# Staged queries, whole values and an earlier place for the first keys in the second attention's loads

## The chip, the cores and the metric

The kernel runs on one core of one Trainium2 chip. The metric is the device time of one execution in microseconds. Three runs of the kernel before gave 2737.96, 2739.23 and 2741.26 us, so its median is 2739.23 us. Lower is better.

## The reference

The program is a network of two blocks over 1024 tokens of width 1024, all in fp32. The first block is a short-convolution layer and a stick-breaking attention layer. The second block, which the change concerns, is this (cut):

```
h = rmsnorm(x) * (1 + scale1) + shift1
qa, ka, va, qd, kd, vd, ga, gd = split(h @ w_in)     # 512,128,128,512,512,512,1024,1024 columns
# sliding window attention: 8 query heads, 2 key/value heads, head size 64, window 128
scores = qa . ka * 64**-0.5 - slope * distance;  softmax with a sink logit;  out_a = probs . va
# differential attention: 4 heads, two score maps each, value size 128
a = softmax(map 0) - lam * softmax(map 1);  out_d = rmsnorm(a . vd) * (1 - lam_init)
x = x + gate1 * ((sigmoid(ga) * (out_a @ w_branch_swa) + sigmoid(gd) * (out_d @ w_branch_diff)) @ w_out)
```

After it come a feed-forward part with a causal convolution, and a last rmsnorm.

## The kernel before, in words

Activations lie transposed, features on the partitions and tokens along the row. A product in fp32 is made of three passes of two rounded parts: each operand is split into a high and a low part, and high x high, low x high and high x low are added in PSUM. So most tensors exist twice, as part 0 (high) and part 1 (low).

**The projections of the second block (`U_IN2`).** The first four column blocks are ordinary products. The thirty others are made in 15 blocks i = 0 to 14 of two units (row 0 and row 1), each by seven products of half-size matrices, in TensorE's order P1, P2, P6, P5, P7, P4, P3. ScalarE takes copies of PSUM between them (`snap`, L2324): number 0 after P1, number 1 after P6, number 2 after P7. P6 waits for copy 0, P7 for copy 1, and P3 waits for a sum of VectorE (L3017) that reads copy 2. ScalarE's whole order is written out by hand in `in2_act`: it also makes the high parts of the weights (L2296) and of the results (`in2_use`, L2358), and it issues the stores of the results (`in2_store`, L2370 and after) on its own DMA queue. VectorE makes the low part of a result (`in2_low`, L3028) before its store.

The queries are units 0 to 7 in storing order. Units of the four ordinary products are stored first: in `in2_act` two calls of `in2_store(-2, row)` stand together ahead of `snap(0, 2)`, and two calls of `in2_store(-1, row)` together ahead of `snap(1, 0)`. The query units 4 to 7 are stored in blocks 1 and 2, row 0 ahead of `snap(i, 2)` and row 1 behind it. Each store writes one part of one unit, [128, 1024], into `q2_dram[part, 128 rows, :]`; a unit's 128 rows are two heads of 64. Before the stage of `in2_use` is written again it waits for the stores of the same row.

**The second attention.** TensorE, ScalarE, VectorE and GpSimd walk through 16 steps of sliding window attention (a head and a half of the tokens each: step x is head x // 2, half x % 2) and then 32 steps of differential attention. In step t, TensorE makes the scores of step t (L854), turns the probabilities of step t - 2 (L893) and multiplies those of step t - 3 with the values (L912). VectorE makes the minimum and the biased scores of step t (L1152) and after them the norm of step t - 1 (L1204). ScalarE makes the exponentials (L1029).

The queries of head pair c lie in `opA[:, e, c, :]`, e being the head of the pair. The upper 64 partitions hold the low part and the lower 64 the high part, and the keys (`keys[slot][part]`) hold the same 64 rows twice, so that one matmul over 128 partitions adds two of the three passes. The values of key/value head g are wanted in a form with 128 columns a block, one half of them zero: head n reads `vals[2 * g + n % 2]`, in which the values stand in half n % 2 and the other half is zero (written by GpSimd, L1669, in `second_pool`).

**The queue of loads.** All loads of this attention are issued by SyncE in the order of `second_loads`, on one queue. It waits for P1 of the last block, issues the first half of the tokens of pairs 0 to 3 (L684, 16 transfers of 64 partitions), waits for P7 of the last block and a low weight of VectorE, issues two pieces more, the first keys (`dup`, L638, four transfers of 64 partitions and 4 KB a row) and the values (L663, two transfers in pieces of 64 numbers), then waits for P4, and issues the other second halves. The keys and values of group 1, the queries of the differential heads and their keys follow. TensorE's step 0 waits for the first half of pair 0 and for the first keys, its step 1 for the second half of pair 0 (`q_half`, L843). Gates are stored by ScalarE (L2377) in the same stretch, on the other queue.

Of the kernel before, what the change touches and what calls it, by code (L numbers as in the profile page):

```python
# [10 lines left out]
F32 = mybir.dt.float32  # L11
# [5 lines left out]
P = 128  # L17
T = 1024
D = 1024
# [275 lines left out]
def program(nc, a, out, known):  # L295
# [3 lines left out]
    with ctx:  # L299
# [10 lines left out]
        def at(name, offset, shape, dt=F32):  # L310
            return nc.alloc_sbuf_tensor_at(name, [P] + shape, dt, offset=offset)
# [67 lines left out]
        def scratch(name, shape, dt=F32):  # L379
            return nc.dram_tensor(name, shape, dt).ap()  # L380
# [2 lines left out]
        k_dram = scratch("k_dram", [2, D, T])  # L383
        q_dram = scratch("q_dram", [2, D, T])
        v_dram = scratch("v_dram", [KC, P, T])
        q2_dram = scratch("q2_dram", [2, D, T])
        k2_dram = scratch("k2_dram", [2, D, T])
        va_dram = scratch("va_dram", [P, T])
        vd_dram = scratch("vd_dram", [DIFF_HEADS, P, T])
# [182 lines left out]
        def now(s):  # L572

            return total.get(id(s), 0)

        def step(s, *name, by=1):

            total[id(s)] = now(s) + by
            if name:
                names[name] = now(s)  # L580
# [52 lines left out]
        def second_loads(sp):  # L633
            def dup(slot, hf, rows, name, cols_of):

                for part in range(2):
                    for place in range(2):
                        sp.dma_start(keys[slot][part][place * DH:(place + 1) * DH, cols_of].bitcast(F32),  # L638
                                     k2_dram[part, rows, cols_of]).then_inc(k_in[slot][hf], 16)
                        step(k_in[slot][hf], *name, by=16)  # L640

            def diff_keys(q):
                j, m = diff_map(q)
                slot = key_slot(q)
                if q == 1:
                    sp.wait_ge(pe_done, at("seven", U_IN2, LAST_IN2, P3))
                elif q < 3:
                    sp.wait_ge(pe_done, at("sec_S", 4 * q + 7, 0))
                else:
                    former, fm = diff_map(q - 3)  # L650
                    sp.wait_ge(pe_done, at("sec_S", SWA_STEPS + NT * former + NT - 1, fm))
                rows = slice((1 + j) * P + m * DH, (1 + j) * P + m * DH + DH)
                for hf in range(2):
                    dup(slot, hf, rows, ("k_in", "diff", q, hf), slice(hf * HALF, (hf + 1) * HALF))

            def swa_keys_values(g):
                if g:
                    sp.wait_ge(pe_done, at("seven", U_IN2, LAST_IN2, P3))
                dup(g, 0, slice(g * DH, (g + 1) * DH), ("k_in", "swa", g), slice(0, T))
                for e in range(2):  # L660
                    dst = vals[2 * g + e][:].rearrange("p (b s d) -> p b s d", b=NT, s=2)[:, :, e, :]
                    src = va_dram.rearrange("p (b s d) -> p b s d", b=NT, s=2)[:, :, g, :]
                    sp.dma_start(dst, src).then_inc(v_in[g], 16)  # L663
                    step(v_in[g], "v_in", "swa", g, by=16)

            def diff_value(j):
                x = 8 * j + 7
                sp.wait_ge(pe_done, at("sec_pv", x, second_pieces(x) - 1))
                sp.dma_start(vals[2 * (j % 2)][:], vd_dram[j]).then_inc(v_in[j % 2], 16)
                step(v_in[j % 2], "v_in", "diff", j, by=16)  # L670

            def queries(c):

                for e in range(2):
                    for part in range(2):
                        sp.dma_start(opA[part * DH:(part + 1) * DH, e, c, :].bitcast(F32),
                                     q2_dram[part, c * P + e * DH:c * P + (e + 1) * DH, :]).then_inc(q_in[c], 16)
                        step(q_in[c], "q_in", c, by=16)

            def query_half(c, e, hf):  # L680

                t = slice(hf * HALF, (hf + 1) * HALF)
                for part in range(2):
                    sp.dma_start(opA[part * DH:(part + 1) * DH, e, c, t].bitcast(F32),  # L684
                                 q2_dram[part, c * P + e * DH:c * P + (e + 1) * DH, t]).then_inc(q_half[c][hf], 16)
                    step(q_half[c][hf], "q_half", c, hf, by=16)

            def branch_weights(n):

                u = U_BRANCH + n  # L690
                for w, col0, row0, chunks, k0 in source(u):
                    src = w[row0:row0 + chunks * P, col0:col0 + P].rearrange("(k p) n -> p k n", p=P)
                    sp.dma_start(branch_raw(n)[:, k0:k0 + chunks, :], src).then_inc(w_in[u % 2], 16)
                    step(w_in[u % 2], "w_in", u, by=16)


            sp.wait_ge(in2_stored[0], at("in2_stored", U_IN2 + 16))
            sp.wait_ge(in2_stored[1], at("in2_stored", U_IN2 + 17))
            sp.wait_ge(pe_done, at("seven", U_IN2, LAST_IN2, P1))
            for c in range(4):  # L700
                for e in range(2):
                    query_half(c, e, 0)
            sp.wait_ge(pe_done, at("seven", U_IN2, LAST_IN2, P7))
            sp.wait_ge(dve_done, at("seven_w", U_IN2, LAST_IN2, P3))
            query_half(0, 0, 1)
            swa_keys_values(0)
            sp.wait_ge(pe_done, at("seven", U_IN2, LAST_IN2, P4))
            query_half(0, 1, 1)
            for c in range(1, 4):
                for e in range(2):  # L710
                    query_half(c, e, 1)

            sp.wait_ge(pe_done, at("seven", U_IN2, LAST_IN2, P3))
            swa_keys_values(1)
            for j in range(DIFF_HEADS):
                queries(4 + j)
            diff_keys(1)
            diff_keys(0)
            diff_value(0)
            diff_keys(2)  # L720
            for row in range(2):
                sp.wait_ge(in2_stored[row], at("in2_stored", in2_unit(LAST_IN2, row)))
            for n in range(2):
                branch_weights(n)
            for n in EARLY_GATES:
                sp.dma_start(gates[:, n, :], gate_dram[n]).then_inc(gates_in, 16)
                step(gates_in, "gates_in", by=16)
            for j in range(1, DIFF_HEADS):
                diff_value(j)
                diff_keys(2 * j + 1)  # L730
                if j < DIFF_HEADS - 1:
                    diff_keys(2 * j + 2)
# [797 lines left out]
        def _(pool):  # L1530
# [106 lines left out]
            def second_pool():  # L1637
# [22 lines left out]
                for g in range(2):  # L1660
                    if g:
                        pool.wait_ge(pe_done, at("seven", U_IN2, LAST_IN2, P3))
                    else:
                        pool.wait_ge(pe_done, at("seven", U_IN2, LAST_IN2, P5))
                        pool.wait_ge(dve_done, at("seven_w", U_IN2, LAST_IN2, P3))
                    for e in range(2):
                        other = vals[2 * g + e][:].rearrange("p (b s d) -> p b s d", b=NT, s=2)[:, :, 1 - e, :]
                        pool.wait_ge(pool_done, now(pool_done))
                        pool.memset(other, 0.0).then_inc(pool_done, 1)  # L1669
                        step(pool_done, "val_zero", g)  # L1670

                row = bias[:, 0, :]
                pool.wait_ge(dve_done, at("sec_p", SWA_STEPS - 2, 0))
# [414 lines left out]
        def _(act):  # L2088
# [272 lines left out]
            def in2_store(i, row):  # L2361

                u = in2_unit(i, row)
                n = in2_place(u)
                act.wait_ge(act_done, at("in2_used", u))
                if in2_kind(u) == "parts":
                    act.wait_ge(dve_done, at("in2_lo", u))
                    dram, row0 = (q2_dram, n * P) if n < 8 else (k2_dram, (n - 8) * P)
                    for part in range(2):
                        act.dma_start(halves_of(dram[part, row0:row0 + P, :]), in2_stage(row, part).bitcast(F32)).then_inc(in2_stored[row], 16)  # L2370
                        step(in2_stored[row], "in2_stored", u, by=16)
                elif in2_kind(u) == "value":
                    dst = va_dram if n == 13 else vd_dram[n - 14]
                    act.dma_start(halves_of(dst), in2_plain(row)).then_inc(in2_stored[row], 16)
                    step(in2_stored[row], "in2_stored", u, by=16)
                else:
                    act.dma_start(halves_of(gate_dram[n - 18]), in2_plain(row)).then_inc(in2_stored[row], 16)  # L2377
                    step(in2_stored[row], "in2_stored", u, by=16)
# [891 lines left out]
```

## Time and profile before

| what | value |
|---|---|
| median of 3 runs | 2739.23 us (2737.96 to 2741.26) |
| profiled execution, its own time | 2738.89 us |
| its span | 2737.1 us |
| mean granted TensorE clock | 0.978 |
| PE (TensorE) busy | 2598.2 us, 95% of the span |
| DVE (VectorE) busy | 1531.7 us, 56% |
| ACT (ScalarE) busy | 1109.5 us, 41% |
| POOL (GpSimd) busy | 857.6 us, 31% |
| queue q1 (SyncE's) | 303.91 MB, 37.3% of 16 engines' span |
| queue q10 (ScalarE's) | 68.69 MB, 6.7% |

Busy time is an average over stages with different limits. Whether an edit counts is read from the place where it lies: which wait ends last there. "ACTq" and "SPq" in a row are the sequencers of ScalarE and SyncE issuing a DMA. While a sequencer issues, the instructions behind it on its engine stand. The number in square brackets is the time that the engine sat idle before the instruction, with the one that released it.

### The profile page before, as it was taken

How to read it: one execution, taken by the hardware profiler on the slowest of the kernel's cores; microseconds unless marked ns; L12 is line 12 of the kernel's file. 1: busy time of each engine (PE TensorE's matmuls, PEld its weight loads, DVE VectorE, ACT ScalarE, POOL GpSimd, SP SyncE). 2: the span in 40 equal slices, each digit the busy share in tenths (PEclk: the TensorE clock that was granted, in tenths of full speed). 3: DMA queues.
4: the chain of work that ended last, by engine and by line, in shares of the span. 5: the costliest groups of instructions: out<-in, count | busy, mean ns of one | idle time of the engine just before them, and what ended most of it. 6: DMA issues, size and time to landing. Idle time of an engine off the chain costs nothing.

```text
span 2737.1 us, 34710 instructions
## 1 busy us (share of the span) xinstructions
PE 2598.2 (95%) x12391; PEld 2161.8 (79%) x12391; DVE 1531.7 (56%) x2083; ACT 1109.5 (41%) x1865; POOL 857.6 (31%) x627
## 2 busy tenths in 40 slices
PE   6999999999899999999899988889997999999998
PEld 4888887788788899987688878668776888887887
DVE  5665665630424566657853438766578777771112
ACT  5200102511410688846544437661265555551000
POOL 2233331032232566620222220333101322325664
PEclk8999999999999999999999999999998999999999
DMA  6344444262455544434353346414242333338833
GB/s 242 100 142 136 143 134 123 77 222 86 146 197 168 126 111 109 112 119 154 103 176 115 109 149 169 152 32 169 85 131 93 102 115 108 108 106 306 288 94 122
DMA packets 377272, 374.81 MB, mean 137 GB/s; under 512 B 36323, under 2 KB 284556, under 8 KB 376972
## 3 DMA queue, kind: packets, MB, share of 16 engines
q1 hardware_dynamic: 346844, 303.91, 37.3%
q10 hardware_dynamic: 30256, 68.69, 6.7%
q8 instruction: 99, 1.62, 0.3%
q14 instruction: 73, 0.60, 0.1%
HBM read 286.55 MB, written 85.98 MB: 136 GB/s over the span
## 4 chain that ended last, share of the span: by engine, by line
PE 76%; DVE 12%; ACT 4%; DMA 3%; issue 1%; SPq 1%; POOL 1%; ACTq 0%; DVEq 0%; POOLq 0%
PE PS L1773 28%; PE PS L1861 20%; PE PS L1930 8%; PE PS L810 5%; PE PS L1820 3%; PE PS L788 2%; PE PS L2001 2%; DMA mod_raw<-in_w_ada 1%; PE PS L774 1%; PE PS L773 1%; DVE prob L1185 1%; PE PS L1843 1%; PE PS L1975 1%; DVE M L2659 1%; DVE Xr L2981 1%
## 5 line engine op out<-in xcount | busy, mean ns | idle before, releaser
L1773 PE MATMUL PS<-opA,w_hi 128*128 128x512 f32 x2176 | 680.2, 392 | 3.0 <-POOL w_lo L1579 3.0
L1773 PEld LDWEIGHTS PS<-opA,w_hi 128*128 128x128 f32 x2176 | 411.1, 189 | 89.3 <-POOL w_lo L1579 3.4
L1773 PE MATMUL PS<-opA,w_lo 128*128 128x512 f32 x1088 | 425.4, 391 | 0.0
L1574 POOL CAST w_hi<-w_raw 128x1024 fp32r<-128x1024 f32 (+1 forms) x117 | 123.4, 1055 | 793.2 <-PE PS L1773 448.2
L1861 PE MATMUL PS<-opB,Xr 128*128 128x512 f32 x1120 | 312.1, 396 | 17.4 <-ACT M L2324 17.4
L1579 POOL TENSOR_TENSOR w_lo<-w_raw,w_hi 128x1024 fp32r<-128x1024 f32 (+1 forms) x118 | 285.2, 2417 | 34.8 <-ACT w_hi L2203 25.4
L1861 PE MATMUL PS<-opA,Xr 128*128 128x512 f32 x980 | 277.2, 393 | 6.2 <-ACT M L2324 3.0
L1861 PEld LDWEIGHTS PS<-opB,Xr 128*128 128x128 f32 x1120 | 214.7, 192 | 64.2 <-ACT M L2324 18.6
L2659 DVE SCALAR_TENSOR_TENSOR M<-mod_raw,small,M 128x512 f32<-128x512 f32 x168 | 177.6, 1057 | 139.5 <-DMA mod_raw<-in_w_ada 80.4
L1773 PEld LDWEIGHTS PS<-opA,w_lo 128*128 128x128 f32 x1088 | 205.6, 189 | 42.4 <-issue 0.2
L1861 PEld LDWEIGHTS PS<-opA,Xr 128*128 128x128 f32 x980 | 183.0, 188 | 50.1 <-ACT M L2324 8.3
L2943 DVE SCALAR_TENSOR_TENSOR X<-PS,mod,X 128x512 f32<-128x512 f32 x64 | 48.0, 751 | 293.8 <-PE PS L1930 206.5
L1861 PE MATMUL PS<-opA,w_first 128*128 128x512 f32 x840 | 197.8, 391 | 5.6 <-ACT M L2334 5.6
L1861 PEld LDWEIGHTS PS<-opA,w_first 128*128 128x128 f32 x840 | 158.8, 189 | 39.1 <-ACT M L2334 6.0
L1747 POOL TENSOR_TENSOR X<-w_raw 128x512 f32<-128x512 f32 x36 | 48.4, 1344 | 380.0 <-DVE xn L2732 228.2
L1773 PE MATMUL PS<-opB,w_hi 128*128 128x512 f32 x512 | 161.4, 394 | 5.4 <-DVE opB L2931 3.0
L1129 DVE TENSOR_TENSOR_SCAN M<-PS,beta 128x896 f32<-128x896 f32 (+7 forms) x86 | 116.4, 1359 | 69.7 <-ACT PS L1005 55.8
L3017 DVE TENSOR_TENSOR M<-M,PS 128x512 f32<-128x512 f32 x140 | 96.3, 688 | 101.0 <-ACT M L2324 66.1
L2981 DVE TENSOR_TENSOR Xr<-X,Xr 128x512 fp32r<-128x512 f32 x140 | 116.9, 835 | 63.4 <-ACT Xr L2296 55.2
L1930 PE MATMUL PS<-opA,w_hi 128*128 128x512 f32 x480 | 149.3, 389 | 0.0
L2219 ACT ACTIVATE squares<-X 128x512 f32<-128x512 f32 x48 | 30.4, 633 | 236.8 <-DVE X L2943 233.6
L2324 ACT ACTIVATE M<-PS 128x512 f32<-128x512 f32 x105 | 62.8, 598 | 151.8 <-PE PS L1861 127.8
(266 smaller groups left out, 4777.5 us busy)
## 6 DMA issues: line engine op xcount, KB each, us to landing
mod_raw<-in_w_ada SPq DMA_DIRECT2D x96, 256.0 KB, 2.9
z_dram<-opB ACTq DMA_DIRECT2D x44, 512.0 KB, 3.9
w_raw<-in_a_w_in SPq DMA_DIRECT2D x32, 512.0 KB, 4.5
hin<-q_dram SPq DMA_DIRECT2D x64, 256.0 KB, 6.0
w_raw<-in_w_down SPq DMA_DIRECT2D x32, 512.0 KB, 3.9
opA<-z_dram SPq DMA_DIRECT2D x60, 256.0 KB, 5.3
mod_raw<-in_b_mod_w SPq DMA_DIRECT2D x48, 256.0 KB, 2.9
X<-x_dram SPq DMA_DIRECT2D x24, 512.0 KB, 5.9
```

The costliest lines, as they stand in the source:

```text
L810: ins = pe.matmul(PS[:, o, q0 + cols_of.start:q0 + 2 * P], head_v[s][:, kb * P:(kb + 1) * P], a_T[i // 2][kb // NQ][:, kb % NQ, cols_of], ...
L1129: dve.tensor_tensor_scan(rest[n % FACTORS][:, 0:w][:, ::-1], stick_z(n)[:, ::-1], beta[n % BETAS][:, 0:w][:, ::-1], 1.0, ALU.mult, ALU.byp ...
L1574: pool.tensor_copy(hi, raw).then_inc(pool_done, 1)
L1579: pool.tensor_tensor(lo, raw, hi.bitcast(F32), ALU.subtract).then_inc(pool_done, 1)
L1773: ins = pe.matmul(ps, w[:, k0 + k, :], rhs(part, k0 + k), start=(k == 0 and n == 0), stop=(k == chunks - 1 and n == 2))
L1820: ins = pe.matmul(PS[:, bank(v, hf), :], weight(v, w, k), op_in[:, part, k, hf * HALF:(hf + 1) * HALF], start=(k == 0 and n == 0), stop=(k ...
L1861: ins = pe.matmul(PS[:, seven_bank(i, which), :], seven_weight(q, i, which, w)[:, c * P:(c + 1) * P], token_part(which, part, c), start=(s ...
L1930: ins = pe.matmul(PS[:, down_bank(hf, n), :], w[:, s, k, :], z_operand(hf, g, part, k), start=(g == 0 and k == 0 and m == 0), stop=(g == 2 ...
L2324: act.activation(block_tile(q, i, 1)[:, 0:HALF] if n == 2 else M[1][:, n * HALF:(n + 1) * HALF], PS[:, seven_bank(i, P1), :], ACT.Copy).th ...
L2659: dve.scalar_tensor_tensor(out=acc, in0=mod_raw[:, n % 2, :], scalar=c, in1=acc, op0=ALU.mult, op1=ALU.add).then_inc(dve_done, 1)
L2981: dve.tensor_tensor(seven_weight(q, i, which, 1), seven_source(i, which), seven_weight(q, i, which, 0).bitcast(F32), ALU.subtract).then_in ...
L3017: dve.tensor_tensor(tile[:, hf * HALF:(hf + 1) * HALF], former, PS[:, seven_bank(i, which), :], ALU.add).then_inc(dve_done, 1)
```

## The change

- `q2_dram` becomes [8, 128, 2, 1024]: for a head pair c, row p is already the partition of `opA`, and the two heads stand beside each other in the row. A store of one part of a query unit is two transfers, one for each head, of 64 partitions (`in2_store`). The stores of keys stay as they are.
- The queries of a pair are loaded by one transfer over 128 partitions: 512 KB for a half of the tokens (where four of 128 KB stood), 1 MB whole (where four of 256 KB stood).
- The values of a key/value head pair are loaded whole into `vals[3 * g]`, one transfer over 128 partitions. GpSimd zeroes one half of `vals[1 + g]` ahead of it, and after it has landed copies the other head's half over and zeroes that half in the loaded tile.
- In the queue, only the first halves of pairs 0 and 1 stand before the wait for P7. The first keys and values come right behind it, then the first halves of pairs 2 and 3, and after the wait for P4 the four second halves.

```diff
--- before.py
+++ after.py
@@ -383,7 +383,7 @@
         k_dram = scratch("k_dram", [2, D, T])
         q_dram = scratch("q_dram", [2, D, T])
         v_dram = scratch("v_dram", [KC, P, T])
-        q2_dram = scratch("q2_dram", [2, D, T])
+        q2_dram = scratch("q2_dram", [KC, P, 2, T])
         k2_dram = scratch("k2_dram", [2, D, T])
         va_dram = scratch("va_dram", [P, T])
         vd_dram = scratch("vd_dram", [DIFF_HEADS, P, T])
@@ -657,11 +657,8 @@
                 if g:
                     sp.wait_ge(pe_done, at("seven", U_IN2, LAST_IN2, P3))
                 dup(g, 0, slice(g * DH, (g + 1) * DH), ("k_in", "swa", g), slice(0, T))
-                for e in range(2):
-                    dst = vals[2 * g + e][:].rearrange("p (b s d) -> p b s d", b=NT, s=2)[:, :, e, :]
-                    src = va_dram.rearrange("p (b s d) -> p b s d", b=NT, s=2)[:, :, g, :]
-                    sp.dma_start(dst, src).then_inc(v_in[g], 16)
-                    step(v_in[g], "v_in", "swa", g, by=16)
+                sp.dma_start(vals[3 * g][:], va_dram).then_inc(v_in[g], 16)
+                step(v_in[g], "v_in", "swa", g, by=16)
 
             def diff_value(j):
                 x = 8 * j + 7
@@ -671,19 +668,14 @@
 
             def queries(c):
 
-                for e in range(2):
-                    for part in range(2):
-                        sp.dma_start(opA[part * DH:(part + 1) * DH, e, c, :].bitcast(F32),
-                                     q2_dram[part, c * P + e * DH:c * P + (e + 1) * DH, :]).then_inc(q_in[c], 16)
-                        step(q_in[c], "q_in", c, by=16)
-
-            def query_half(c, e, hf):
+                sp.dma_start(opA[:, :, c, :].bitcast(F32), q2_dram[c]).then_inc(q_in[c], 16)
+                step(q_in[c], "q_in", c, by=16)
+
+            def query_half(c, hf):
 
                 t = slice(hf * HALF, (hf + 1) * HALF)
-                for part in range(2):
-                    sp.dma_start(opA[part * DH:(part + 1) * DH, e, c, t].bitcast(F32),
-                                 q2_dram[part, c * P + e * DH:c * P + (e + 1) * DH, t]).then_inc(q_half[c][hf], 16)
-                    step(q_half[c][hf], "q_half", c, hf, by=16)
+                sp.dma_start(opA[:, :, c, t].bitcast(F32), q2_dram[c, :, :, t]).then_inc(q_half[c][hf], 16)
+                step(q_half[c][hf], "q_half", c, hf, by=16)
 
             def branch_weights(n):
 
@@ -697,18 +689,16 @@
             sp.wait_ge(in2_stored[0], at("in2_stored", U_IN2 + 16))
             sp.wait_ge(in2_stored[1], at("in2_stored", U_IN2 + 17))
             sp.wait_ge(pe_done, at("seven", U_IN2, LAST_IN2, P1))
-            for c in range(4):
-                for e in range(2):
-                    query_half(c, e, 0)
+            query_half(0, 0)
+            query_half(1, 0)
             sp.wait_ge(pe_done, at("seven", U_IN2, LAST_IN2, P7))
             sp.wait_ge(dve_done, at("seven_w", U_IN2, LAST_IN2, P3))
-            query_half(0, 0, 1)
             swa_keys_values(0)
+            query_half(2, 0)
+            query_half(3, 0)
             sp.wait_ge(pe_done, at("seven", U_IN2, LAST_IN2, P4))
-            query_half(0, 1, 1)
-            for c in range(1, 4):
-                for e in range(2):
-                    query_half(c, e, 1)
+            for c in range(4):
+                query_half(c, 1)
 
             sp.wait_ge(pe_done, at("seven", U_IN2, LAST_IN2, P3))
             swa_keys_values(1)
@@ -1663,11 +1653,19 @@
                     else:
                         pool.wait_ge(pe_done, at("seven", U_IN2, LAST_IN2, P5))
                         pool.wait_ge(dve_done, at("seven_w", U_IN2, LAST_IN2, P3))
-                    for e in range(2):
-                        other = vals[2 * g + e][:].rearrange("p (b s d) -> p b s d", b=NT, s=2)[:, :, 1 - e, :]
-                        pool.wait_ge(pool_done, now(pool_done))
-                        pool.memset(other, 0.0).then_inc(pool_done, 1)
-                        step(pool_done, "val_zero", g)
+                    parts_of = "p (b s d) -> p b s d"
+                    whole = vals[3 * g][:].rearrange(parts_of, b=NT, s=2)
+                    other = vals[1 + g][:].rearrange(parts_of, b=NT, s=2)
+                    pool.wait_ge(pool_done, now(pool_done))
+                    pool.memset(other[:, :, g, :], 0.0).then_inc(pool_done, 1)
+                    step(pool_done)
+                    pool.wait_ge(v_in[g], at("v_in", "swa", g))
+                    pool.wait_ge(pool_done, now(pool_done))
+                    pool.tensor_copy(other[:, :, 1 - g, :], whole[:, :, g, :]).then_inc(pool_done, 1)
+                    step(pool_done)
+                    pool.wait_ge(pool_done, now(pool_done))
+                    pool.memset(whole[:, :, 1 - g, :], 0.0).then_inc(pool_done, 1)
+                    step(pool_done, "val_zero", g)
 
                 row = bias[:, 0, :]
                 pool.wait_ge(dve_done, at("sec_p", SWA_STEPS - 2, 0))
@@ -2365,10 +2363,16 @@
                 act.wait_ge(act_done, at("in2_used", u))
                 if in2_kind(u) == "parts":
                     act.wait_ge(dve_done, at("in2_lo", u))
-                    dram, row0 = (q2_dram, n * P) if n < 8 else (k2_dram, (n - 8) * P)
                     for part in range(2):
-                        act.dma_start(halves_of(dram[part, row0:row0 + P, :]), in2_stage(row, part).bitcast(F32)).then_inc(in2_stored[row], 16)
-                        step(in2_stored[row], "in2_stored", u, by=16)
+                        for e in range(2 if n < 8 else 0):
+                            d = slice(e * DH, (e + 1) * DH)
+                            act.dma_start(halves_of(q2_dram[n, part * DH:(part + 1) * DH, e, :]),
+                                          in2_stage(row, part)[d].bitcast(F32)).then_inc(in2_stored[row], 16)
+                            step(in2_stored[row], "in2_stored", u, by=16)
+                        if n >= 8:
+                            act.dma_start(halves_of(k2_dram[part, (n - 8) * P:(n - 7) * P, :]),
+                                          in2_stage(row, part).bitcast(F32)).then_inc(in2_stored[row], 16)
+                            step(in2_stored[row], "in2_stored", u, by=16)
                 elif in2_kind(u) == "value":
                     dst = va_dram if n == 13 else vd_dram[n - 14]
                     act.dma_start(halves_of(dst), in2_plain(row)).then_inc(in2_stored[row], 16)
```

## Rows read from the trace of the kernel before

**Rows 1.** The page's part 4, the chain that ended last, by engine.

```profile
PE 76%; DVE 12%; ACT 4%; DMA 3%; issue 1%; SPq 1%; POOL 1%; ACTq 0%; DVEq 0%; POOLq 0%
```

**Rows 2.** Timeline, 1344 to 1364: start us, us, engine, line, count [idle before].

```profile
1347.47 3.49 ACTq L2370 DMA_DIRECT2D q_dram<-opB  x4
...
1351.14 0.60 ACT L2324 ACTIVATE M<-PS 128x512 f32<-128x512 f32 x1 [3.11 <-PE PS L1861]
...
1352.57 3.01 PE L1861 MATMUL PS<-opA,Xr 128*128 128x512 f32 x12 [1.55 <-DVE M L3017]
...
1359.11 3.47 ACTq L2370 DMA_DIRECT2D q_dram<-opB  x4
...
1363.35 7.34 PE L1861 MATMUL PS<-opB,Xr 128*128 128x512 f32 x24 [2.33 <-ACT M L2324]
```

**Rows 3.** The chain, 1335 to 1450: start us, us, what.

```profile
1349.68 1.28 ACTq L2370
...
1359.12 2.14 DVE opB L3028
...
1361.34 0.52 ACTq L2370
...
1361.89 0.68 ACTq L2370
...
1363.35 83.50 PE PS L1861 x360
```

**Rows 4.** DMA issues by line: count, ns min/median/max, first and last start.

```profile
L2370 ACTq DMA_DIRECT2D q_dram<-opB x16: 520/636/1282, 1347.5 to 1393.1; - x16
...
L638 SPq DMA_DIRECT2D keys<-k_dram x72: 444/597/1590, 1627.6 to 1803.3; - x72
...
L669 SPq DMA_DIRECT2D vals<-vd_dram x4: 320/326/352, 1681.4 to 1780.7; - x4
```

**Rows 5.** Window after TensorE's stop: busy us by engine, PEclk, DMA share, GB/s.

```profile
1363.30:1366.00 2.70, 2.65 (x7) 2.06 (x8) 2.36 (x4) 2.33 (x3) 0.15 (x1) 0.56 1.04 338
```

**Rows 6.** Timeline of ScalarE, 1370 to 1377.

```profile
1373.44 0.60 ACT L2324 ACTIVATE M<-PS 128x512 f32<-128x512 f32 x1 [2.04 <-PE PS L1861]
...
1374.84 0.63 ACT L2296 ACTIVATE Xr<-X 128x512 fp32r<-128x512 f32 x1 [0.79 <-DVE M L3017]
```

**Rows 7.** Timeline, 1590 to 1680, around the start of the second attention.

```profile
1614.60 12.96 SPq L684 DMA_DIRECT2D opA<-q_dram  x18
...
1622.73 1.11 POOL L1669 MEMSET vals<- 128x512 f32 x2 [8.80 <-PE PS L1861]
...
1625.42 0.60 ACT L2324 ACTIVATE M<-PS 128x512 f32<-128x512 f32 x1 [4.84 <-PE PS L1861]
...
1627.60 2.52 SPq L638 DMA_DIRECT2D keys<-k_dram  x4
...
1634.51 0.52 ACTq L2377 DMA_DIRECT2D gate_dram<-opBf  x1
...
1635.77 2.47 PE L854 MATMUL PS<-keys,opA 128*128 128x128 f32 x10 [4.95 <-DMA keys<-k_dram]
...
1640.92 4.21 PE L854 MATMUL PS<-keys,opA 128*128 128x256 f32 x18 [2.68 <-DMA opA<-q_dram]
...
1646.47 1.97 PE L893 MATMUL PS<-ident,prob 128*128 128x128 f32 x8 [1.34 <-DVE prob L1204]
```

**Rows 8.** Windows (GB/s last): X loads; mixed; 64-partition loads; before step 1.

```profile
1189.00:1193.00 4.00, 4.00 (x20) 3.30 (x19) 1.73 (x2) 1.95 (x3) 0.00 (x0) 1.00 1.03 422
1637.00:1640.00 3.00, 1.25 (x6) 0.95 (x5) 1.68 (x9) 0.00 (x0) 0.00 (x0) 0.50 1.06 406
1658.00:1668.00 10.00, 9.25 (x82) 8.96 (x81) 8.09 (x38) 8.15 (x25) 0.00 (x0) 1.00 1.03 245
1626.90:1640.90 14.00, 6.40 (x28) 5.12 (x26) 3.06 (x11) 4.26 (x6) 1.05 (x2) 0.73 1.10 294
```

**Rows 9.** The page's part 5, GpSimd's cast of a weight.

```profile
L1574 POOL CAST w_hi<-w_raw 128x1024 fp32r<-128x1024 f32 (+1 forms) x117 | 123.4, 1055 | 793.2 <-PE PS L1773 448.2
```

## The prediction

> **What bounds the kernel now.** I read the chain of waits first: it lies on TensorE for 76% of the span [rows 1]. A change in loads and stores can therefore move the time only where TensorE stands still near it. The timeline shows two such places.
>
> The first is the beginning of the seven-product stage, where the queries are stored. TensorE stands still 1.55 us before 1352.57 and 2.33 us before 1363.35. Each stop ends with a PSUM copy by ScalarE (L2324, `snap`), which stands behind a run of four query stores on ScalarE's own sequencer [rows 2]. The chain runs through these issues: 1.28 us for the fourth of the first run, 0.52 and 0.68 us for the last two of the second [rows 3]. After 1363.35 the chain stays on TensorE for 83.50 us [rows 3], so whatever is added in front of that point isn't won back.
>
> The second is the start of the second attention. TensorE's last product ends at 1630.8. It waits 4.95 us for the first keys (scores of step 0 at 1635.77), and then 2.68 us for the second half of the first queries (step 1 at 1640.92). The first turned probabilities follow at 1646.47 [rows 7].
>
> **The stores: four issues become eight in each run.** The first query units, stored ahead of the first ordinary product, are written in runs of two rows by two parts, so 4 issues a run (16 in all, two runs and then four pairs). The change cuts each into two issues of 64 partitions.
>
> The cost of one such issue isn't in the trace. On ScalarE an issue of 128 partitions in two halves takes 0.520 us at least and 0.636 us in the median. On SP one of 64 partitions takes 0.597 us, and one of 128 whole partitions 0.326 us, so halving the partitions doesn't make an issue cheaper there [rows 4]. Lower bound: 0.52 us. Upper bound: 0.52 + (0.597 - 0.326) = 0.79 us. I take 0.64 us, nearest to the median of the same line and to SP's row, and 0.04 us between issues.
>
> First run: it starts at 1347.47, and eight issues take 8 x 0.68 = 5.4 us where four took 3.49, so +1.9 us (bounds: 8 x 0.56 = 4.5, +1.0; 8 x 0.83 = 6.6, +3.2). Behind it stands `snap` at 1351.14, then VectorE's sum and TensorE's P3 at 1352.57 [rows 2]. That `snap` waits only for P7, which TensorE had done before P4 began; its cover is already gone (TensorE stands still), so all 1.9 us count. All that leads to the second run shifts with it.
>
> Second run: row 0's four issues begin at 1359.11 and must end before row 1's low part, ready at 1361.3 [rows 2, 3]. 4 x 0.68 = 2.7 us end 0.5 us too late. Row 1's four then take 2.7 us where two took 1.2 us [rows 3]. Together +2.0 us (bounds: +1.0 and +3.3) on the `snap` that P6 of the next block waits for.
>
> The later four pairs: in the first of them ScalarE idles 2.04 us before its copy at 1373.44, and the two added issues (1.4 us) fit in that. Behind the next pair stands a weight copy at 1374.84 for a product of the next block, which TensorE reaches after four others [rows 6]. I price these at nothing; without that cover each pair would cost 1.4 us.
>
> Clock: after the 2.33 us stop the granted clock is 0.56 over 1363.3 to 1366 [rows 5], which is the lower level, 1.2 GHz, for most of it. The stops grow to about 3.5 and 4.3 us. A stretch at the lower level in P1 and P2 of block 1 is hidden by the second stop, which ScalarE's chain sets. A longer one after the second stop isn't: I put 0.5 us (bounds 0 and 1.7, one more stretch like the one seen).
>
> **The loads.** SP's wait for P7 ends at about 1625.4 (ScalarE's copy of it starts at 1625.42). Before, SP was still issuing its 18 query pieces (1614.60 to 1627.56), and the keys began at 1627.60 [rows 7]. Now only two issues precede that wait, so the keys go 2.15 us earlier, and step 0's scores run near 1633.4. But nothing is won by that alone. VectorE's order is probabilities of step 1, then the norm of step 0, then TensorE turns step 0. The turning at 1646.47 hangs on step 1, thus on the second half of the first queries, which takes 5.55 us from its landing to the turning [rows 7].
>
> Where is that piece now? Behind four key transfers, the whole values, and the first halves of pairs 2 and 3 (1 MB that moved before the keys until now). The queue is full in this stretch: 294 GB/s at a DMA share of 1.10 from 1626.9 to 1640.9 [rows 8]. Rates: transfers to 64 partitions run at 245 GB/s (1658 to 1668), to 128 partitions at 422 (1189 to 1193), reads and gate stores mixed at 406 (1637 to 1640) [rows 8]. From 1626.9, the new order has to move:
> - keys, 1.05 MB at 250 GB/s, with the gate store issued at 1625.4 beside them: 4.3 us (5.7 if they don't overlap);
> - values, 0.52 MB at 422 GB/s: 1.2 us;
> - three query transfers (1.57 MB) and the last two gate stores (1.05 MB, the last issued at 1634.51 [rows 7]) at 406 GB/s: 6.5 us.
>
> This is 12.0 us, to 1638.9. The same arithmetic on the old order (0.52 MB of queries and the gate store at 406 GB/s 2.6 us, keys 4.2, values at the keys' rate 2.1, two gate stores and the last query piece 2.9) gives 1638.7, where the trace has 1640.92. So both carry 2.2 us of latency and mixing, and the new landing is 1641.1: +0.2 us. Bounds: -2.6 us if the query pieces pass the gate stores (1.57 MB at 422 GB/s is 3.7 us instead of 6.5), +1.6 us if keys and gate store don't overlap. A delay or gain here passes on whole, since from 1646.47 each step follows the one before it; the other loads of this attention are on time by many us and stay so.
>
> The Trainium skill ("SBUF — State Buffer", the section on the DMA port swizzle) says that a transfer over 64 partitions reaches only half of the SBUF ports and so half of the bandwidth. The 245 against 422 GB/s of rows 8 agree for loads. The rule speaks against this change at its other end: the new stores cover 64 partitions each. By it, a run's 2.1 MB would take 8.6 us (at 245 GB/s) instead of 5.0 (at 422), and land up to 3.6 us later. ScalarE's next high part waits for that landing, but VectorE reads it some 3 us after it is there, so by the page the sum grows by at most half a microsecond, which the upper bounds hold.
>
> **GpSimd.** Per group one memset goes, and a copy and a memset come behind the landing of the values. A memset of this size takes 0.55 us (1.11 for two) [rows 7], a cast of twice the size 1.06 us [rows 9]; so about 1.1 us, done near 1637, some 14 us before step 0's values are wanted. The second group's pair falls beside VectorE's work near 1656: 0 (bounds 0 and 0.5). What is queued behind, the second bias, waits for step 14.
>
> **Sum** against the profiled execution (2738.89 us with a span of 2737.1): +1.9 + 2.0 + 0.5 + 0.2 = +4.6, thus 2743.5. The median of the runs stands 0.34 us above the profiled one: 2743.8 us.
>
> **Rivals.**
> - *Slower.* Half-partition issues cost 0.79 us, and the two stops lengthen enough for one more stretch at the lower clock: 3.2 + 3.3 + 1.7 + 0.2 = +8.4, 2747.6 us. Place: ScalarE's sequencer ahead of the two `snap` copies. It passes the 0.2% named below when an issue costs over about 0.69 us (two runs, 16 issues: 16 x 0.05 = 0.8 us more). For it: both runs are already on the chain, and the fourth issue took 1.28 us. Against: that 1.28 us looks like a queue that was full, and smaller transfers fill it less.
> - *The stores are free.* An issue may cost by its descriptors, and each new one has half as many; then eight cost what four did. With half of the loads' lower bound: about 2738.0 us. Against: SP's rows, where 64 descriptors cost more than 128.
> - *The loads pay.* If the query piece landed as soon as step 0's scores are done (1635.8), step 1 would start 5.1 us earlier. With free stores this is 2734.1, with mine 2738.5 (the clock's 0.5 included). Against: the bytes ahead of it.
> - *The keys don't come earlier or it doesn't matter:* inside the forecast, since only step 1 counts.
>
> **Chances.** Forecast 0.50, slower rival 0.34, free stores 0.11, loads that pay 0.05. A difference of 0.2% is about what a measurement of this kernel tells from none; it lies at 2733.8 and 2744.7. My forecast stands 0.9 us inside it. A little of its own spread lies above and a little of the slower rival's below; so faster 0.06, same 0.57, slower 0.37. Range 2738.0 to 2748.5: the low end is the free stores and lies just under all low bounds together (+1.0 + 1.0 - 2.6 = -0.6, 2738.6), the high end is the slower rival with 0.9 us of the loads' upper bound.
>
> **What would show it.** In the new trace: query stores in 64-partition issues of 0.6 to 0.7 us; TensorE's stops before P3 of block 0 at about 3.5 us and before P6 of block 1 at about 4.3 us, both behind ScalarE's copy; keys issued at 1625.4 plus the shift; step 0's scores about 2.4 us nearer to the last product; step 1's scores 10 us after the last product, as now. Wrong if the stops stay at 1.5 and 2.3 us, or if step 1 starts more than 2 us nearer or farther.

## The result, and where the time went

| kernel | median of its runs | beside it, before | ratio, 95% interval |
|---|---|---|---|
| changed | 2750.38 us (2747.18 to 2751.62, 5 runs) | 2741.26 us (5 runs) | 1.0033 [1.0022, 1.0044] |

The change makes the kernel slower by 9.0 us (0.33% of 2741). The forecast was 2743.8 us with a range up to 2748.5, so the time lies outside it. The direction is that of the slower rival (2747.6 us). Part of the gap is the starting point: the forecast counts from 2739.23 us, and the kernel before, run beside the changed one, gave 2741.26. As a difference the forecast was +4.6 us, with bounds up to +9.3, against +9.0 measured. Differences in us here are the ratio less one, times the median beside it.

The first view is the timeline at the beginning of the seven-product stage, with ScalarE's issues ("ACTq"), its PSUM copy and TensorE's stops. It answers to [rows 2]:

```profile
1348.40 6.79 ACTq L2369 DMA_DIRECT2D q_dram<-opB  x8
...
1355.36 0.60 ACT L2322 ACTIVATE M<-PS 128x512 f32<-128x512 f32 x1 [6.41 <-issue]
...
1356.79 5.49 PE L1859 MATMUL PS<-opA,Xr 128*128 128x512 f32 x12 [4.43 <-DVE M L3021]
...
1363.33 7.97 ACTq L2369 DMA_DIRECT2D q_dram<-opB  x8
...
1372.07 7.38 PE L1859 MATMUL PS<-opB,Xr 128*128 128x512 f32 x24 [3.91 <-ACT M L2322]
```

The first run of issues takes 6.79 us (3.49 before), the second 7.97 (3.47 before, with a pause in it for row 1's low part; in the changed kernel that part is ready in time). The stop before P3 is 4.43 us (1.55 before). The first run begins 0.93 us later than before, for the reason given next. From the start of that run to the 24 products of P6 the distance grows from 1363.35 - 1347.47 = 15.88 us to 1372.07 - 1348.40 = 23.67 us: 7.8 us. In between, the 12 products of P3 take 5.49 us instead of 3.01, since TensorE's clock stands at its lower level, 1.2 GHz, after the longer stop (granted clock 0.50 from 1356.8 to 1362). That is why the second stop alone, 3.91 us, looks small: part of the wait went by in slower products. ScalarE's own chain shows where the 7.8 us lie: 3.3 in the first run of issues (6.79 - 3.49), 4.5 from the start of the second run to P6 (1372.07 - 1363.33 = 8.74, against 1363.35 - 1359.11 = 4.24), and nothing in the 8.1 us between the two runs. So the slower products of P3 cost nothing themselves. The 0.93 us ahead of the run is such a stretch too, in an earlier product, and has no part of the change in it (with the new stores alone it was 0.23 us).

The chain of waits shows the single issues of the two runs (start us, us), as in [rows 3]:

```profile
1349.76 0.70 ACTq L2369
...
1350.49 0.97 ACTq L2369
...
1353.33 1.04 ACTq L2369
...
1363.33 0.58 ACTq L2369
...
1368.85 2.44 ACTq L2369
...
1372.07 83.55 PE PS L1859 x360
```

The first three issues of a run take 0.58 to 0.70 us, the later ones 0.64 to 1.04, and the last of the second run 2.44 us. Over all query stores (count, ns least/median/most), against [rows 4]:

```profile
L2369 ACTq DMA_DIRECT2D q_dram<-opB x32: 582/764/2438, 1348.4 to 1404.6; - x32
```

The windows (the last two columns are DMA share and GB/s) show how fast the bytes move. In the kernel before, and in the changed one, five microseconds from the first run on:

```profile
1349.00:1354.00 5.00, 3.45 (x15) 2.54 (x15) 1.94 (x3) 2.54 (x4) 0.00 (x0) 1.00 1.03 382
```

```profile
1350.00:1355.00 5.00, 2.37 (x11) 1.63 (x9) 0.00 (x0) 0.00 (x0) 0.00 (x0) 1.00 0.89 258
```

The stores move at 258 GB/s instead of 382, at a DMA share of 0.89. In the first full microsecond of the movement the rate is about half of the old one, with the DMA engines as busy:

```profile
1349.00:1350.00 1.00, 1.00 (x6) 0.81 (x6) 0.00 (x0) 0.00 (x0) 0.00 (x0) 1.00 1.03 381
```

```profile
1350.00:1351.00 1.00, 1.00 (x6) 0.84 (x5) 0.00 (x0) 0.00 (x0) 0.00 (x0) 1.00 0.99 197
```

So the transfers themselves are slow. They don't merely start late.

The second place is the start of the second attention, which answers to [rows 7]:

```profile
1623.36 1.23 SPq L677 DMA_DIRECT2D opA<-q_dram  x2
...
1634.18 2.74 SPq L638 DMA_DIRECT2D keys<-k_dram  x4
...
1637.62 3.83 SPq L677 DMA_DIRECT2D opA<-q_dram  x6
...
1642.64 2.27 PE L844 MATMUL PS<-keys,opA 128*128 128x128 f32 x10 [3.06 <-DMA keys<-k_dram]
...
1643.84 0.61 POOL L1664 COPY vals<-vals 128x512 f32<-128x512 f32 x1 [11.82 <-DMA vals<-va_dram]
...
1649.29 4.09 PE L844 MATMUL PS<-keys,opA 128*128 128x256 f32 x18 [4.37 <-DMA opA<-q_dram]
...
1654.83 1.09 PE L883 MATMUL PS<-ident,prob 128*128 128x128 f32 x8 [1.45 <-DVE prob L1194]
```

TensorE's last product ends at 1639.58 (1642.64 - 3.06). Step 0's scores begin 3.06 us behind it instead of 4.95, since the keys come earlier. Step 1's begin 9.71 us behind it instead of 10.10. So the loads give 0.4 us, and not the 1.9 us of the keys: the second half of pair 0 decides. Up to the first turning this execution is 8.4 us behind the profiled one of the kernel before (1654.83 - 1646.47): 0.9 + 7.8 - 0.4. The other 3.7 us or so between the two executions lie behind it and weren't traced.

### The profile page after: what moved, and what is told of

Read it like the earlier page. It is cut to its first block, busy times and chain, and to the rows that moved or that the text cites. A ratio compares the mean times of both kernels' runs of the same rounds, so it can differ in the third digit from the quotient of the medians.

```text
span 2749.2 us, 34692 instructions
## 1 busy us (share of the span) xinstructions
PE 2602.5 (95%) x12391; PEld 2162.3 (79%) x12391; DVE 1535.2 (56%) x2083; ACT 1110.1 (40%) x1865; POOL 862.3 (31%) x629
## 4 chain that ended last, share of the span: by engine, by line
PE 78%; DVE 10%; ACT 4%; DMA 3%; issue 1%; ACTq 1%; POOL 1%; SPq 1%; DVEq 0%; POOLq 0%
PE PS L1771 28%; PE PS L1859 22%; PE PS L1928 8%; PE PS L800 5%; PE PS L1818 3%; PE PS L778 2%; PE PS L1999 2%; DMA mod_raw<-in_w_ada 1%; PE PS L764 1%; PE PS L763 1%; DVE prob L1175 1%; PE PS L1841 1%; DVE M L2663 1%; PE PS L1973 1%; DVE w_lo L2764 1%
```

## Experiments

Each ran with the kernel before on the same chip. Ratios are to that kernel, with their 95% intervals. The code shown is cut to what matters ("...").

**The new stores alone.** The kernel before, with the layout and the stores of the change:

```diff
-act.dma_start(halves_of(dram[part, row0:row0 + P, :]), in2_stage(row, part)...)
+act.dma_start(halves_of(q2_dram[n, part * DH:(part + 1) * DH, e, :]), in2_stage(row, part)[d]...)  # e = 0, 1
-sp.dma_start(opA[part * DH:..., e, c, t], q2_dram[part, c * P + e * DH:..., t])
+sp.dma_start(opA[part * DH:..., e, c, t], q2_dram[c, part * DH:(part + 1) * DH, e, t])
```

> The kernel before with only the new layout of the queries in DRAM and the new stores (two issues of 64 partitions for each part of a query unit). Loads, queue order and values are as before; the four query transfers of a pair read the new layout. Theory A (the stores cost it all, on ScalarE's sequencer ahead of the two PSUM copies): +7 to +9 us, and TensorE's stops at the two places near 4.4 and 3.9 us, as in the changed kernel. Rival B (stores cost the forecast 4.4 us, and the rest is in the loads or GpSimd): +4 to +5 us.

Measured: 2750.17 us against 2740.53, ratio 1.0034 [1.0022, 1.0047], thus +9.3 us (6.0 to 12.9). The whole loss is here, as far as the intervals tell. The timeline of ScalarE's issues has the same two runs:

```profile
1347.70 6.83 ACTq L2371 DMA_DIRECT2D q_dram<-opB  x8
1362.69 7.91 ACTq L2371 DMA_DIRECT2D q_dram<-opB  x8
...
1371.37 8.51 PE L1861 MATMUL PS<-opB,Xr 128*128 128x512 f32 x24 [4.85 <-ACT M L2324]
```

From the first run to P6 it is 23.67 us again. Here the 24 products behind the second stop take 8.51 us instead of 7.34: the granted clock is at its lower level, 0.50, up to 1377. These 1.2 us add to the 7.8. In this execution the start of the attention is also 1.5 us longer than before (the first keys are waited for 6.52 us, not 4.95). In the run with 64 partitions and the old rows, below, it is 0.1 us longer, so it isn't counted for the stores.

**The new loads alone.** The changed kernel with one store of 128 partitions for each part:

```diff
-for e in range(2): act.dma_start(halves_of(q2_dram[n, part * DH:(part + 1) * DH, e, :]), in2_stage(row, part)[d])
+rows = q2_dram[n].rearrange("p e t -> (p e) t")
+act.dma_start(halves_of(rows[part * P:(part + 1) * P, :]), in2_stage(row, part))
```

> The changed kernel with the query stores as before, one issue of 128 partitions for each part. The rows then lie in DRAM in the order of the old stores, so the queries that the attention reads are permuted; the same bytes move. Theory A: the time of the kernel before within 2 us (-0.5 us by the start of the attention), stops of 1.5 and 2.3 us, an issue of 0.52 to 1.3 us. Rival B: +3 to +5 us over before.

Measured: 2741.03 us against 2740.53, ratio 0.9996 [0.9988, 1.0005]. Loads, queue order, whole values and GpSimd's copies together are worth nothing that can be told from zero (-3.3 to +1.4 us). The start of the attention is as in the changed kernel (view of waits: engine and line, releaser, us in total, times, longest):

```profile
PE PS L844 <- DMA opA<-q_dram: 4.2, 1, 4.2
PE PS L844 <- DMA keys<-k_dram: 3.1, 1, 3.1
```

**Count or width?** Three kernels separate what is slow in the new stores. The first has as many issues, each over 128 partitions and half of the tokens:

```diff
-for e in range(2): act.dma_start(..., in2_stage(row, part)[d])                # 64 partitions, two halves
+for h in range(2): act.dma_start(rows[part * P:(part + 1) * P, h * HALF:(h + 1) * HALF], in2_stage(row, part)[:, h, :])
```

> The changed kernel with as many query stores, each over 128 partitions and half of the tokens instead of 64 partitions and all tokens: the same bytes and the same 32 issues. The rows are permuted as in e2. If the number of issues costs, the two runs take as long as in the changed kernel (6.8 and 8.0 us) and the time is +7 us or more over before. If transfers of 64 partitions are slow and pace the issues (258 GB/s in the first run against 382 before), the issues take 0.52 to 0.65 us each, the runs 4.5 to 5.5 us at about 380 GB/s, and the time is +3 to +5 us over before.

Measured: 2742.71 us, ratio 1.0007 [0.9998, 1.0016], thus +1.9 us with an interval that reaches zero. The runs and the rate are as expected, the time is less than the +3 to +5 us that was:

```profile
1350.57 4.48 ACTq L2370 DMA_DIRECT2D q_dram<-opB  x8
1363.21 4.46 ACTq L2370 DMA_DIRECT2D q_dram<-opB  x8
```

```profile
1352.00:1356.00 4.00, 2.15 (x10) 1.45 (x8) 0.08 (x1) 0.65 (x2) 0.00 (x0) 1.00 1.02 383
```

Eight issues take 4.5 us at 383 GB/s. Doubling their number adds 1.0 us to each run; this is the lower bound of the forecast. The time is about a fifth of what the change costs. In this execution the 24 products of P6 take 5.73 us instead of 7.34, so 1.6 us of clock came back; the time of a single execution isn't firmer than that.

The issues are cheaper from the first on:

```profile
1350.57 0.34 ACTq L2370
...
1350.94 0.46 ACTq L2370
```

In the changed kernel the first issues of the two runs take 0.68 and 0.58 us, for the same 256 KB. So this kernel doubles the number at a lower price for each issue. At 0.62 us an issue and 0.04 us between them eight would take 5.3 us (an estimate). The number alone is thus worth 1.0 us a run as measured, and up to 1.8 us at the old price.

The second has 64 partitions, but the old rows in DRAM:

```diff
+for e in range(2): act.dma_start(halves_of(dram[part, row0 + e * DH:row0 + (e + 1) * DH, :]), in2_stage(row, part)[d])
```

> The kernel before with each query store cut into two of 64 partitions, in the old layout (the rows lie one behind the other in DRAM). If 64 partitions on the SBUF side are what is slow: as in the run with the new stores alone, +7 to +10 us, first run of issues 6.5 to 7 us, about 260 GB/s. If the DRAM rows 8 KB apart of the new layout are what is slow: runs of 4.5 us at 380 GB/s, +1 to +3 us.

Measured: 2749.46 us against 2740.83, ratio 1.0035 [1.0021, 1.0049], thus +9.6 us, as with the new stores. The rate over 1349 to 1354 is 262 GB/s. The first issues of the two runs take 0.58 and 0.52 us, where those over 128 partitions took 0.59 and 0.52 in the kernel before; it is the later ones that grow, to 0.96 us at the fourth of the first run and 1.01 at the sixth.

```profile
1347.60 6.76 ACTq L2372 DMA_DIRECT2D q_dram<-opB  x8
1362.50 7.90 ACTq L2372 DMA_DIRECT2D q_dram<-opB  x8
```

The third has 128 partitions, and rows 8 KB apart as in the new layout:

```diff
+dst = q2_dram[n, :, part, :]
+act.dma_start(halves_of(dst), in2_stage(row, part))
```

> The changed kernel with one store of 128 partitions for each part (16 query stores), into every second 4 KB row of the new layout. The queries that the attention reads are permuted; the same bytes move. 64 partitions slow: runs of 3.5 us as before, the time of the kernel before within 2 us. DRAM rows slow: runs of over 5 us, +4 us or more.

Measured: 2739.20 us, ratio 0.9995 [0.9986, 1.0004].

```profile
1345.67 3.11 ACTq L2368 DMA_DIRECT2D q_dram<-opB  x4
1356.94 3.19 ACTq L2368 DMA_DIRECT2D q_dram<-opB  x4
```

The layout in DRAM costs nothing. The first run of the changed kernel takes 6.8 us; the number of issues accounts for 4.5 to 5.3 of them, against 3.5 before, and the rest, 1.5 to 2.3 us, comes with the 64 partitions on the SBUF side. In the second run the rest is 2.7 to 3.5 us. By the times of the kernels the number gives 1.9 us and the 64 partitions the remaining 7 to 8, but the price of an issue differs between them, so this division is the less firm one. Why the first issues of the first and of the third kernel are cheap (0.34 and 0.37 us) wasn't found.

**The stores behind the copies.** The changed kernel, each run of eight moved behind the `snap` it stood ahead of:

```diff
-for row in range(2): in2_store(-2, row)
 snap(q, 0, 2)
+for row in range(2): in2_store(-2, row)
```

(and the same with `in2_store(-1, row)` and `snap(q, 1, 0)`).

> The changed kernel, with each run of eight query stores placed behind ScalarE's PSUM copy instead of ahead of it. If the cost is that the copy stands behind the issues, TensorE's stop before P3 of block 0 goes (0 to 1 us) and the time falls by 5 us at least, against the changed kernel, some of it given back where the next high parts stand behind the stores. If the cost is the transfers themselves (ScalarE waiting for landings before it may write the stage again), it falls by less than 2 us.

Measured: 2747.49 us against 2740.53, ratio 1.0029 [1.0020, 1.0039]. This expectation missed. By the ratios the time is 7.9 us over the kernel before, where the changed kernel is 9.0 over it; the intervals overlap, so no gain is shown. The stop before P3 is gone (no wait is shown there), the one before P6 is 2.41 us, and a new one stands before P7, behind the copy between them, which now has the second run of issues ahead of it:

```profile
1364.82 8.32 ACTq L2369 DMA_DIRECT2D q_dram<-opB  x8
```

```profile
1378.98 1.06 ACT L2356 ACTIVATE opB<-M 128x1024 fp32r<-128x1024 f32 x1 [2.42 <-DMA q_dram<-opB]
...
1380.80 1.22 PE L1859 MATMUL PS<-opA,Xr 128*128 128x512 f32 x2 [8.08 <-ACT M L2322]
```

The second branch of the expectation is thus in part right too: ahead of that copy ScalarE also waits 2.42 us for a store to land (0.47 us in the kernel before) until it may write the stage again. ScalarE has three copies and nine high parts (seven of weights, two of results) to make in each block of some 19 us. In the two places tried a run of 7 to 8 us was too long; the move only chose which product waits.

**The first pieces first.** The stores and 64-partition pieces of the kernel before, whole values, and this order:

```diff
-for c in range(4): (first halves);  wait P7;  query_half(0, 0, 1);  keys and values
-wait P4;  query_half(0, 1, 1)
+for c in range(3): (first halves);  wait P7;  keys;  query_half(0, 0, 1)
+wait P4;  query_half(0, 1, 1);  values whole;  first half of pair 3
```

> The stores and 64-partition query pieces of the kernel before, values whole with GpSimd's copy, and an order in which nothing stands between the first keys and the second half of pair 0: first halves of pairs 0 to 2, wait for P7, keys, second half of pair 0 around the wait for P4, values, the rest. If step 1 of the attention hangs on the bytes ahead of its query piece, as the forecast said: keys land about 2 us earlier, step 1's scores begin 3 to 4.5 us earlier against the last product (near 6 us behind it instead of 10), and the time is 3 to 4.5 us under the kernel before. If the start hangs on something else (latency of a landing, clock): less than 1 us.

Measured: 2736.54 us against 2740.83, ratio 0.9984 [0.9976, 0.9993], thus 4.4 us under the kernel before, as expected.

```profile
1628.40 2.73 SPq L638 DMA_DIRECT2D keys<-k_dram  x4
...
1631.17 2.53 SPq L681 DMA_DIRECT2D opA<-q_dram  x4
...
1637.02 4.18 PE L855 MATMUL PS<-keys,opA 128*128 128x128 f32 x18 [3.21 <-DMA keys<-k_dram]
...
1645.47 1.97 PE L894 MATMUL PS<-ident,prob 128*128 128x128 f32 x8 [1.32 <-DVE prob L1205]
```

The 18 score products of steps 0 and 1 stand in one group: step 1 no longer waits for its queries in this execution. From the last product (1633.81) to the first turning it is 11.66 us; it was 15.65 (1646.47 - 1630.82), and 15.25 in the changed kernel (1654.83 - 1639.58). So the earlier start is there to be had with the old stores and the old query pieces. The kernel differs from the one before in the order and in the whole values; the two weren't tried apart.

**And the first run of stores behind.** The same with the four (old) stores of the first run behind `snap(q, 0, 2)`.

> The one with the first pieces first, and the first run of four query stores placed behind ScalarE's copy of P7. The stop of 1.55 us before P3 of block 0 goes, but ScalarE's next high parts stand behind the stores instead, so the stop before P6 of block 1 grows by about as much: 0 to 1 us under the one without it.

Measured: 2732.84 us, ratio 0.9969 [0.9956, 0.9981], the fastest here: 8.5 us under the kernel before. Against the one without the move it is 3.7 us by the medians, more than the 0 to 1 us that was expected; the two intervals overlap (0.9976 to 0.9981), so the size of this difference is not firm.

```profile
1349.37 2.88 PE L1870 MATMUL PS<-opA,Xr 128*128 128x512 f32 x12
...
1360.48 5.74 PE L1870 MATMUL PS<-opB,Xr 128*128 128x512 f32 x24 [2.78 <-ACT M L2333]
...
1366.79 0.73 PE L1870 MATMUL PS<-opA,Xr 128*128 128x512 f32 x2 [0.57 <-ACT M L2333]
```

The stop of 1.55 us is gone, the next is 2.78 instead of 2.33 us, and the 24 products behind it take 5.74 us instead of 7.34 (in the kernel before, and also in the one without the move): in this execution the clock stayed at its upper level, 2.4 GHz. So about 1.6 us of the gain is clock, which isn't sure to come in each execution, and 0.5 us is the stop less what came back (0.45 before P6, and 0.57 before P7). Another 1.1 us lies at the start of the attention, 10.60 us from the last product to the first turning instead of 11.66:

```profile
1630.20 1.39 PE L855 MATMUL PS<-keys,opA 128*128 128x128 f32 x10 [2.98 <-DMA keys<-k_dram]
...
1632.28 4.21 PE L855 MATMUL PS<-keys,opA 128*128 128x256 f32 x18 [0.68 <-DMA opA<-q_dram]
```

Step 0's ten score products take 1.39 us, where they took 2.47 before [rows 7]; that is the clock too, and step 1 waits 0.68 us for its queries again. The rest wasn't traced to a place.

## Why the prediction was wrong

**The place was right.** Both runs of stores stand on the chain ahead of the two copies, nothing hides them, and all of the loss is there. The later four pairs were priced at nothing; the chain behind the second run is one piece of TensorE, 83.55 us against 83.50 [rows 3], so that held.

**The price of an issue in a run failed.** The step reads: "I take 0.64 us, nearest to the median of the same line and to SP's row". The first three issues of a run do take 0.58 to 0.70 us, so for them the value was good. But it was used for eight in a row. The runs took 6.8 and 8.0 us, that is 0.85 and 1.0 us an issue, above the 0.68 of the sum and the 0.83 of its upper bound (0.79 and 0.04 between issues). The bound was built from the issue times of other transfers, most of them over 128 partitions. With the number alone doubled, the runs take 4.5 us (5.3 by the estimate above) and the cost is 1.9 us; with 64 partitions they take 6.8 and 7.9 us, and it is 9 us. Term by term, in the profile of the changed kernel: the first run cost 3.3 us, not 1.9; the second 4.5, not 2.0 (both just or clearly past their upper bounds, 3.2 and 3.3); the clock behind the second stop nothing, not 0.5. In the two other kernels with such stores in the same places (the new stores alone, and 64 partitions with the old rows) that last term was 1.2 us, and the stores then come to 9.0 and 8.9 us, which agrees with the medians (+9.3 and +9.6).

**The row for it was on the table.** The forecast read 245 against 422 GB/s for 64 and 128 partitions [rows 8], used it for the loads, and then set the same fact aside for the stores: it asked only when the stores land, and not whether slower transfers hold up the issues behind them. The fourth issue of the run before had taken 1.28 us, and the text called that a queue that was full. It then reasoned that smaller transfers fill it less. They are smaller, but they drain more slowly, and a run's 2.1 MB are the same. That the later issues wait for room in the queue is not shown: it fits that the first issue is no dearer over 64 partitions than over 128 (0.58 and 0.52 us against 0.59 and 0.52, in the same rows), and that the issues grow within a run while the DMA engines move the bytes slowly, but no run here looked into the queue. What is shown is that a run of issues over 64 partitions takes longer, in four kernels, than its number and the rows in DRAM account for. In the second run two weight loads of SyncE are issued from 1368.27 on, and the last store issue, at 1368.85, takes 2.44 us; in the first run, without such loads, the last took 0.78. That these loads slow it further is likely, but it wasn't tried alone.

The Trainium skill's rule ("SBUF — State Buffer", the section on the DMA port swizzle: a transfer over 64 partitions reaches half of the ports) was cited with the verdict that it hardly changes the sum. By the times of the kernels the width of the stores was the largest term. The trace agrees with half in the first full microsecond, 197 against 381 GB/s; over five microseconds, with stores from both halves of the partitions in turn, it is 258 against 382, two thirds. The estimate made from the rule also asked only for the landing. The one landing that ScalarE's high parts waited longer for (1.75 us in the changed kernel, 0.47 before) made no product wait, so that part of the step held.

**The loads.** The step "the new landing is 1641.1: +0.2 us" came out at -0.4 us, with keys 1.9 us earlier and step 1's query piece where it was. That the order behind the keys decides was right: with the piece moved up, 4.4 us are won (4.0 of them between the last product and the first turning, by the profile).

**GpSimd.** A copy of 0.61 us at 1643.84 and a memset behind it, for values that the attention takes after its first turning at 1654.83: nothing is seen of it, as forecast.

**The chances.** The slower rival had 0.34, with 8.4 us by a sum of upper bounds. Its place (ScalarE's sequencer ahead of the two copies) is where it happened; its price for an issue was still a little low in the first run and 1.2 us low in the second. The extra stretch of low clock fell where it cost nothing in the changed kernel's profile, and cost 1.2 us in the two others. The range ended 1.9 us short, which is no more than the 2.0 us between the two medians of the kernel before; counted from the later one it would just have held the time.

Not settled: how the +9.0 us of the median divide behind the first turning. Stores and loads add to 7.4 us in the two profiles; the interval, 6.0 to 12.1 us, holds that. Single stretches at the lower clock come and go between executions, and are a likely cause of the rest.

## What to carry to other kernels

Price a run of DMA issues twice, by their number and by bytes over the rate of that shape of transfer, and let the larger be the upper bound. Here 2.1 MB at 258 GB/s are 8.1 us, and the runs took 6.8 and 8.0; at 382 GB/s they are 5.5 us, and the runs took 4.5 (eight issues) and 3.5 (four). An issue that took longer than its neighbours in the old trace is a sign that the second price may count. Cutting a full-width store into two of 64 partitions to make one later load simpler moves the cost to the storing side, where it may stand in a compute engine's order. When a start waits for several transfers, what counts is the bytes that stand ahead of the last one needed, not the place of the first.

## What was not expected of the hardware

A row stride of 8 KB in DRAM cost a store nothing: 3.1 to 3.2 us for a run of four against 3.47 to 3.49, if anything less. Eight issues over 128 partitions with one 2 KB piece a partition took 4.5 us, so such an issue costs 0.56 us in a run, where one of 64 partitions with two pieces costs 0.85 to 1.0, for the same bytes. And the first issue of a run over 64 partitions cost what it did over 128, in the same rows (0.58 and 0.52 us against 0.59 and 0.52); the issues grew later in the run, to 0.97 us at the fourth in the changed kernel.
